# Two branch projections as three products of split operands in place of full fp32 products

## The chip, the cores and the metric

The kernel runs on one core of a Trainium2 chip. The metric is device time in microseconds (us), the median of several executions. One execution was also recorded by the hardware profiler; all rows below come from it. TensorE is called PE, its weight load PEld, VectorE DVE, ScalarE ACT, GpSimd POOL, SyncE SP.

## The reference, cut to what matters

Three layers run one after the other on 512 tokens of width 1024 (with 256 context tokens in the first two). Mixer A is a grouped attention with rotary positions, mixer B a neighbourhood attention; the third layer has two branches side by side, an mLSTM and a sparse attention, and merges them. Only this merge is touched:

```python
ya = sigmoid(p["m_o"]) * mh * silu(p["m_z"])          # 512 x 1024, from the mLSTM
yb = yn * silu(p["n_z"])                              # 512 x 512, from the sparse attention
merged = (sigmoid(p["g_a"]) * (ya @ w_branch_a[l])    # 1024 x 1024
          + sigmoid(p["g_b"]) * (yb @ w_branch_b[l])) # 512 x 1024
x = x + merged @ w_out[l]
```

512 tokens are eight selection blocks, fewer than the sixteen to be selected, so all are taken, and the sparse attention is, for a query tile, two causal attentions over the same past, plus a small one over compressed blocks.

## The kernel before, in words

**Layout.** Activations lie with features on partitions: 8 chunks k of 128 features, each 128x512. Weights come in "units" of 256 output columns (1 MB, eight chunks of 128x256), loaded by SP in the fixed order `UNITS` (line 56 on) into `W`, which holds two units in turn.

**Split products.** For most units the weight and the activation are each held in two parts, a high one rounded to fp32r and a low one, the remainder. ACT casts `W` into `WH` (line 1692), POOL subtracts to get `WL` (line 2431; DVE in a few places), in four pieces per unit. `WH` and `WL` too hold two units in turn (`PART`). The activation's parts lie in `H` (`HX`, `HC`) and `L` (`LX`, `LC`); `parts` makes them, with a cast on ACT (line 1742) and a subtraction on DVE (2038) or POOL (2472). A product over one chunk is then three fp32r matmuls (lines 1416 to 1418): high by high, high by low, low by high. `proj` is this product, `pj` the generator that emits it, eight chunks to one 128x512 output.

**Plain units.** Units named in `PLAIN` are not split: `x_wa` (line 1662, branch A: 4 units x 2 outputs x 8 chunks = 64 products) and `x_wb` (line 1672, branch B: 8 outputs x 4 chunks = 32 products) multiply `W` by the fp32 activation directly. The trace records two MATMULs for each of these full products.

**Order of work.** Every engine runs its part of one list, `plan`, in order; semaphores tie the engines together. `tick` emits the next waiting piece of a split at chunks 3 and 7 of an output, that is four times per unit. `tick` also emits the load of the unit after next when the fourth piece is out; for a plain unit the load is emitted when the unit's products are done. Within an attention (`careful`), a piece waits until its load is some work old.

**The sparse attention stage.** `attention("c", ...)` runs 32 steps (4 head pairs x 4 query tiles x 2 key sets). Step n emits its scores (line 1496), the softmax on DVE (max), ACT (exp) and POOL (scaling), then the output product of step n-2 (lines 1523, 1531) and the transposes of step n-1 (line 1506). There is one pair of score banks, so the scores of step n+1 wait for both exps of step n. Between, `fill_in` takes products from `gen_c`: 16 of gate unit `ga` j, 16 of `wa` j, for j = 0 to 3. Each step has two halves; a half with weight t takes products until the sum `spent` of their declared costs has reached

```python
until_ = spent[0] + (work - spent[0]) * todo[n][2] / left
```

A tile's weight is (tile+1)/2.5. A `ga` product declares 5.12, a `wa` product 9; `work` is 64 x (5.12 + 9) = 903.7.

**After it.** Eight outputs of gate units `gb` (64 products), then branch B with `x_wb` f = 0 to 7, each followed by a DVE multiply (2403), a DVE add (2406) and the parts of `mg` f; then `out_proj("wo")`, the last norm and the stores. `out_proj` starts with seven chunks of two outputs in turn, so chunk 7 of `mg` is needed late.

**The mLSTM.** Per head hd, projections `mq`, `mk`, `mv`, `mo`, `mz`; after some of them `do_later` emits one deferred piece of the head before (`m_den`, `m_var`, `m_scale`). `m_scale` ends with POOL writing `ya` (line 2531).

Of the kernel before, what the change touches and what calls it, by code (L numbers as in the profile page):

```python
# [8 lines left out]
ALU = mybir.AluOpType  # L9
# [63 lines left out]

UNITS = unit_order()
EARLY = [0, 4, 1, 5, 2, 6, 3, 7]
PLAIN = ("mod", "w1k", "w1v", "wa", "wb")
PART = [sum(u[0] not in PLAIN for u in UNITS[:n]) % 2 for n in range(len(UNITS))]


# [87 lines left out]
def build(nc, wu, vp, cc, cs1, xt, biasb, pos, out):  # L167
    ctx = ExitStack()
    with ctx:
# [116 lines left out]
        s_pcs, s_pc, s_pce, s_pct, s_pcT = (signal("cmp_" + n) for n in ("scores", "work", "exp", "turn", "turned"))  # L286
        s_nth, s_nz = signal("n_gate_tanh"), signal("n_gate")

        s_ga, s_wa, s_mg, s_gbt, s_wb, s_mgb, s_sum, s_fin = (signal("x_" + n) for n in ("ga", "wa", "merged_a", "gb", "wb", "merged_b", "merged", "final"))

        plan, before, last = [], {}, {}

        COST = {"proj": 0.6, "score": 1.0, "turn": 0.5, "pv": 0.7, "x_wa": 0.9, "mod_mm": 0.9, "m_qk": 0.9, "m_num": 1.0}
        done_work, loaded_at, careful = [0.0], {}, [False]

        def do(*item):
# [812 lines left out]
        def m_var(hd):  # L1111
            mps["var", hd] = bank(ONE.take(("mvar", hd), (s_vv, (hd,))))
            do("m_var", hd)

        def m_scale(hd):
            mps["hb", hd] = bank(ONE.take(("mhb", hd), (s_hs, (hd, 1))))
            do("m_scale", hd)

        for hd in range(4):
            conv("mq", hd)  # L1120
            do_later(hd)
            conv("mk", hd)
            do_later(hd)
            if hd == 0:
                do("m_decay")
            un = Unit("mv", hd)
            for s in range(4):
                o = bank(ONE.take(("mv", hd, s), (s_vh, (hd, s))))
                run(pjt(("mv", hd, s), un, s, "h", o))
                do("m_value", hd, s)  # L1130
            un.done(s_proj, "mv", hd, 3)
            do_later(hd)
            for nm_ in ("mo", "mz"):
                un = Unit(nm_, hd)
                for m in range(2):
                    g = (nm_, hd, m)
                    o = bank(ONE.take(g, (s_oth, (hd, m)) if nm_ == "mo" else (s_zg, (hd, m))))
                    run(pj(g, un, 0, T, 128 * m, "h", o))
                    do("m_gate", *g)
                un.done(s_proj, *g)  # L1140
                if nm_ == "mo":
                    if hd == 0:
                        for x, ev in (("g", s_gc), ("s", s_em), ("r", s_gb)):
                            mps["gcol", x] = bank(ONE.take(("gcol", x), (ev, ())))
                            do("m_gate_col", x)
                        do("m_gates_done")
                    mps["E", hd] = bank(ONE.take(("mE", hd), (s_ee, (hd, 3))))
                    do("m_exp", hd)
            for j in range(4):
                mps["qk", hd, j] = bank(ONE.take(("mqk", hd, j), (s_sw, (hd, j))))  # L1150
                do("m_qk", hd, j)
            for m in range(2):
                mps["num", hd, m] = bank(ONE.take(("mnum", hd, m), (s_num, (hd, m))))
                do("m_num", hd, m)
            do("m_num_sq", hd)
            later[:] = [lambda hd=hd: m_den(hd), lambda hd=hd: m_var(hd), lambda hd=hd: m_scale(hd)]

# [147 lines left out]
        def gen_c():  # L1307
            for j in range(4):
                un = Unit("ga", j)
                for m in range(2):  # L1310
                    g = ("ga", j, m)
                    o = bank(FC.take(g, (s_ga, (j, m))))
                    yield from pj(g, un, 0, T, 128 * m, "h", o)
                    do("x_ga", j, m)
                un.done(s_proj, "ga", j, 1)
                un = Unit("wa", j)
                for m in range(2):
                    wps["wa", j, m] = (un.n, bank(FC.take(("wa", j, m), (s_mg, (j, m)))))
                    for k in range(8):
                        if k % 4 == 3:  # L1320
                            tick()
                        do("x_wa", j, m, k)
                        yield 9
                    do("x_merge_a", j, m)
                un.done(s_wa, j, 1)

        def steps_c(pair):
            out_ = []
# [9 lines left out]
                    out_.append((lambda: True, make, (tile + 1) / 2.5))  # L1338
            return out_

        attention("c", [s for pair in range(4) for s in steps_c(pair)], SC, TC, PbC, PTbC, OC, gen_c(), 8 * 8 * (T / 100 + 9), lambda n: None)

# [3 lines left out]
        for j in range(4):  # L1348
            un = Unit("gb", j)
            for m in range(2):  # L1350
                g = ("gb", j, m)
                o = bank(ONE.take(g, (s_gbt, (2 * j + m,))))
                run(pj(g, un, 0, T, 128 * m, "h", o))
                do("x_gb", j, m)
                if j == 0 and m == 0:
                    rbroad("c", 0, R1)
                do("norm2_x", 2 * j + m)
            un.done(s_proj, "gb", j, 1)
        for jj in range(2):
            un = Unit("wb", jj)  # L1360
            for j in range(2):
                for m in range(2):
                    f = 4 * jj + 2 * j + m
                    tick()
                    wps["wb", f] = (un.n, j, m, bank(ONE.take(("wb", f), (s_mgb, (f,)))))
                    do("x_wb", f)
                    parts("m", f, 0, mg[:, f, :], [(s_sum, (f,)), (s_proj, ("gb", 3, 1))], "pool")
            un.done(s_wb, f)
        norm("e", Arena(), X_ONLY, [(s_wa, (3, 1))], lambda k, p: [(s_res, ("wo", k, 0))])
        out_proj("wo", None, XONLY, False, "m", ["e"])  # L1370
        close("e", 0, ONE)
        RE = bank(ONE.take("RE", (s_fin, (7,))))
# [26 lines left out]
        def tensor(e, w):  # L1399
            def proj(g, k):  # L1400
# [4 lines left out]
                w.wait_ge(*x_low(G.phase, k, int(G.lo >= T)))  # L1405
                f0, f1, part = 256 * k + G.f0, 256 * k + G.f0 + G.width, PART[G.unit]
                wh, wl = WH[:, part, f0:f1], WL[:, part, f0:f1]
                xh, xl = H.at(k, G.lo, G.hi), L.at(k, G.lo, G.hi)
                if G.by_tokens:
                    o = G.out[:, 0:G.width]  # L1410
                    e.matmul(o, xh, wh, start=(k == 0), stop=False)  # L1411
# [241 lines left out]
                    t = e.transpose(cps["turn", tile][:, 128 * g:128 * g + 128], pc[tile % 2][:, 128 * g:128 * g + 128], c("id"))  # L1653
                t.then_inc(*s_pct.by(tile))

            def x_wa(j, m, k):
                n, o = wps["wa", j, m]
                if k == 0:
                    free(w, ("wa", j, m))
                    w.wait_ge(*s_w[n % 2](n))  # L1660
                    w.wait_ge(*s_ya(3, 1))
                t = e.matmul(o, unit_w(n)[:, k, 128 * m:128 * m + 128], ya[:, k, :], start=(k == 0), stop=(k == 7))  # L1662
                if k == 7:
                    t.then_inc(*s_wa.by(j, m))

            def x_wb(f):
                n, j, m, o = wps["wb", f]
                free(w, ("wb", f))
                w.wait_ge(*s_w[n % 2](n))
                w.wait_ge(*s_post("c", 31))  # L1670
                for k in range(4):
                    t = e.matmul(o, unit_w(n)[:, 4 * j + k, 128 * m:128 * m + 128], nz[:, k, :], start=(k == 0), stop=(k == 3))  # L1672
                t.then_inc(*s_wb.by(f))

            program(e, w, dict(proj=proj, mod_mm=mod_mm, mod_tr=mod_tr, norm_sums=norm_sums, rbroad=rbroad, a_key_sums=a_key_sums,
                               a_key_norm=a_key_norm, a_key_rope=a_key_rope, a_query_sums=a_query_sums, a_query_turn=a_query_turn,
                               score=score, turn=turn, pv=pv, m_gates=m_gates, m_gate_col=m_gate_col, m_exp=m_exp, m_qk=m_qk,
                               m_num=m_num, m_den=m_den, m_var=m_var, m_scale=m_scale, n_rotate=n_rotate, n_hidden=n_hidden,
                               n_cmp_out=n_cmp_out, cmp=cmp, cmp_turn=cmp_turn, x_wa=x_wa, x_wb=x_wb))

        def scalar(e, w):
            def silu():
# [55 lines left out]
            def parts(phase, k, j):  # L1738
                src, after = partsrc[phase, k, j]
                lo, hi = FULL[j]  # L1740
                await_all(w, after)
                e.copy(H.at(k, lo, hi), src).then_inc(*s_xh.by(phase, k, j))

            def a_key_raw(m):
                w.wait_ge(*s_proj("ak", 1, 1))
# [208 lines left out]
        def vector(e, w):  # L1954
# [79 lines left out]
            def parts(phase, k, j):  # L2034
                if part_by[phase, k, j] == "dve":
                    lo, hi = FULL[j]
                    w.wait_ge(*s_xh(phase, k, j))
                    e.tensor_tensor(L.at(k, lo, hi), partsrc[phase, k, j][0], H.at(k, lo, hi).bitcast(F32), ALU.subtract).then_inc(*s_xl_dve.by(phase, k, j))

            def a_key_raw(m):  # L2040
                w.wait_ge(*s_ksq(m))
# [350 lines left out]
                e.scalar_tensor_tensor(out=nz[:, tile, :], in0=nz[:, tile, :], scalar=1.0, in1=groups["nz", tile].out, op0=ALU.add, op1=ALU.mult).then_inc(*s_nz.by(tile))  # L2392

            def x_merge_a(j, m):
                w.wait_ge(*s_wa(j, m))
                w.wait_ge(*s_ga(j, m))
                await_all(w, N_DONE)
                e.scalar_tensor_tensor(out=mg[:, 2 * j + m, :], in0=sg[m], scalar=1.0, in1=wps["wa", j, m][1], op0=ALU.add, op1=ALU.mult).then_inc(*s_mg.by(j, m))

            def x_wb(f):  # L2400
                w.wait_ge(*s_wb(f))
# [20 lines left out]
        def gpsimd(e, w):  # L2422
# [45 lines left out]
            def parts(phase, k, j):  # L2468
                if part_by[phase, k, j] == "pool":
                    lo, hi = FULL[j]  # L2470
                    w.wait_ge(*s_xh(phase, k, j))
                    e.tensor_tensor(L.at(k, lo, hi), partsrc[phase, k, j][0], H.at(k, lo, hi).bitcast(F32), ALU.subtract).then_inc(*s_xl_pool.by(phase, k, j))

            def a_key_sums():
                w.wait_ge(*s_kvar())
# [304 lines left out]
```

## Time and profile before

| what | value |
|---|---|
| median of 3 runs | 1638.17 us (1637.87 to 1638.43) |
| the profiled execution | 1637.83 us |
| its span, first to last instruction | 1636.1 us |
| mean granted TensorE clock | 0.975 |

The profiled execution's own time is 1.7 us above its span. A row of the trace gives start, duration, engine, line, operation, operands and count; "128*128 128x512" is the stationary tile and the moving one. The end of a MATMUL is modelled and includes its way through the array, so neighbouring MATMULs overlap: what one costs PE is the distance from its start to the next start, not its duration.

### The profile page before, as it was taken

To read this page: it belongs to the slowest core of one execution; us is meant where nothing else is said; L and a number is where in the kernel's file an instruction comes from. 1 tells how busy PE (TensorE), PEld (TensorE's weight loads), DVE (VectorE), ACT (ScalarE), POOL (GpSimd) and SP (SyncE) were. 2 spreads that over 40 slices of the span, in tenths; PEclk is the share of its full clock that TensorE was granted. 3 is DMA by queue.
4 is the path that set the end of the run, shared out by engine and by line. 5 is a ranking of instruction groups with operands and counts; after the bars stand their busy time and mean duration, and the time that the engine had idled before them with its cause. 6 is when DMAs were issued, how large, how long until landed. Compare 5 with 4: busy or idle time off the path is not lost.

```text
span 1636.1 us, 25018 instructions
## 1 busy us (share of the span) xinstructions
PE 1559.0 (95%) x9858; PEld 1216.3 (74%) x9858; DVE 733.9 (45%) x1707; ACT 622.4 (38%) x1301; POOL 656.7 (40%) x640
## 2 busy tenths in 40 slices
PE   5899999999898999999999899999999999999997
PEld 3787777777587888787867687878878865655755
DVE  4434555555534345444355563443424444456033
ACT  3244444444532433333344453433322343333221
POOL 2534334444532533434344453525346244333252
PEclk8999999999998999999999899999999999999998
DMA  9111111110132222322231122213122212110221
GB/s 396 36 71 53 44 36 52 52 53 27 53 108 99 82 75 77 110 79 104 78 123 47 61 103 73 86 52 103 52 77 78 91 65 78 52 52 26 78 99 56
DMA packets 22148, 128.20 MB, mean 78 GB/s; under 512 B 2448, under 2 KB 2576, under 8 KB 8080
## 3 DMA queue, kind: packets, MB, share of 16 engines
q1 hardware_dynamic: 21888, 126.35, 21.4%
q8 instruction: 78, 1.28, 0.3%
q14 instruction: 38, 0.31, 0.1%
q10 hardware_dynamic: 144, 0.26, 0.1%
HBM read 124.50 MB, written 2.10 MB: 77 GB/s over the span
## 4 chain that ended last, share of the span: by engine, by line
PE 85%; DVE 6%; ACT 3%; POOL 2%; issue 2%; DMA 1%; SPq 0%; POOLq 0%; DVEq 0%; ACTq 0%
PE PS L1416 16%; PE PS L1418 15%; PE PS L1417 15%; PE PS L1496 7%; PE PS L1506 6%; PE PS L1531 6%; PE PS L1662 3%; PE PS L1411 3%; PE PS L1412 3%; PE PS L1413 3%; PE PS L1672 2%; DVE sm L2110 1%; PE PS L1584 1%; PE PS L1576 1%; PE PS L1429 1%
## 5 line engine op out<-in xcount | busy, mean ns | idle before, releaser
L2431 POOL TENSOR_TENSOR WL<-W,WH 128x512 fp32r<-128x512 f32 x280 | 367.4, 1328 | 321.0 <-ACT WH L1692 320.5
L1416 PE MATMUL PS<-HX,WH 128*128 128x512 f32 x1008 | 421.3, 418 | 9.0 <-DVE LX L2031 3.1
L1418 PE MATMUL PS<-HX,WL 128*128 128x512 f32 x1008 | 399.9, 397 | 0.0
L1417 PE MATMUL PS<-LX,WH 128*128 128x512 f32 x1008 | 399.3, 396 | 0.0
L1416 PEld LDWEIGHTS PS<-HX,WH 128*128 128x128 f32 x1008 | 193.5, 192 | 60.0 <-issue 15.9
L1418 PEld LDWEIGHTS PS<-HX,WL 128*128 128x128 f32 x1008 | 192.7, 191 | 42.9
L1417 PEld LDWEIGHTS PS<-LX,WH 128*128 128x128 f32 x1008 | 193.5, 192 | 37.1 <-issue 3.4
L1692 ACT CAST WH<-W 128x512 fp32r<-128x512 f32 x296 | 172.1, 618 | 48.3 <-DMA W<-in_wu 22.2
L1778 ACT ACTIVATE AR<-PS,sm 128x768 f32<-128x768 f32 (+4 forms) x160 | 115.7, 723 | 171.2 <-DVE sm L2115 101.1
L2110 DVE TENSOR_REDUCE sm<-PS 128x1 f32<-128x512 f32 (+4 forms) x224 | 150.0, 670 | 54.3 <-PE PS L1496 49.7
L2498 POOL TENSOR_SCALAR AR<-AR,sm 128x768 f32<-128x768 f32 (+1 forms) x96 | 75.1, 782 | 186.3 <-DVE sm L2126 186.3
L1496 PE MATMUL PS<-AR 64*128 64x256 f32 (+3 forms) x704 | 124.3, 460 | 9.9 <-ACT XC L1778 4.0
L2498 POOL TENSOR_SCALAR XC<-XC,sm 128x512 f32<-128x512 f32 x64 | 45.0, 704 | 164.2 <-DVE sm L2126 164.2
L1496 PEld LDWEIGHTS PS<-AR 64*128 64x128 f32 x704 | 60.1, 187 | 67.3 <-issue 42.0
L1506 PE MATMUL PS<-C,AR 128*128 128x128 f32 x608 | 100.8, 283 | 7.5 <-DVE AR L2146 3.9
L1788 ACT COPY AR<-PS 128x512 f32<-128x512 f32 (+1 forms) x112 | 62.2, 555 | 118.8 <-PE PS L1506 118.1
L1778 ACT ACTIVATE XC<-PS,sm 128x512 f32<-128x512 f32 x64 | 44.2, 691 | 145.8 <-DVE sm L2115 145.8
L1506 PEld LDWEIGHTS PS<-C,AR 128*128 128x128 f32 x608 | 68.2, 140 | 41.0 <-issue 22.7
L1531 PEld LDWEIGHTS PS<-AR 128*64 128x64 f32 x1408 | 76.0, 137 | 28.3 <-issue 25.2
L1531 PE MATMUL PS<-AR 128*64 128x128 f32 x1408 | 95.4, 280 | 1.5 <-ACT AR L1788 1.2
L1411 PE MATMUL PS<-WH,HX 128*128 128x256 f32 x320 | 94.3, 295 | 0.8 <-POOL WL L2431 0.8
L1413 PE MATMUL PS<-WL,HX 128*128 128x256 f32 x320 | 90.5, 283 | 0.0
(273 smaller groups left out, 2472.6 us busy)
## 6 DMA issues: line engine op xcount, KB each, us to landing
W<-in_wu SPq DMA_DIRECT2D x98, 1024.0 KB, 4.8
AR<-in_wu SPq DMA_DIRECT2D x8, 1024.0 KB, 11.5
AR<-in_biasb SPq DMA_DIRECT2D x32, 256.0 KB, 2.7
XX<-in_xt SPq DMA_DIRECT2D x2, 1024.0 KB, 6.2
out<-XX SPq DMA_DIRECT2D x8, 256.0 KB, 2.2
XC<-in_xt SPq DMA_DIRECT2D x1, 1024.0 KB, 14.3
C<-in_cc SPq DMA_DIRECT2D x1, 770.5 KB, 8.7
CS<-in_cs SPq DMA_DIRECT2D x1, 512.0 KB, 9.6
```

What stands on the lines that cost most here:

```text
L1411: e.matmul(o, xh, wh, start=(k == 0), stop=False)
L1413: t = e.matmul(o, xh, wl, start=False, stop=(k == 7))
L1416: e.matmul(o, wh, xh, start=(k == 0), stop=False)
L1417: e.matmul(o, wh, xl, start=False, stop=False)
L1418: t = e.matmul(o, wl, xh, start=False, stop=(k == 7))
L1496: t = e.matmul(PS[:, s.score[h] + a:s.score[h] + b], l, r, start=True, stop=True)
L1506: t = e.transpose(o[:, j * 128:j * 128 + 128], s.pb[h][:, (q0 + j) * 128:(q0 + j) * 128 + 128], c("id"))
L1531: t = e.matmul(s.out[h], s.values[h][j], s.pt[h][:, j * 128:j * 128 + 128], start=(j == 0 and s.first), stop=(j == nv - 1 and s.final))
L1692: e.copy(WH[:, PART[n], a:z], W[:, n % 2, a:z]).then_inc(*s_wh.by(n, q))
L1778: e.activation(s.pb[h][:, 0:s.n], PS[:, s.score[h]:s.score[h] + s.n], ACT.Exp, bias=smn[:, i % 4:i % 4 + 1], scale=(1.0 if s.scale is None ...
L2110: e.tensor_reduce(mx, x, AX.X, ALU.max).then_inc(*s_max.by(name, n, h))
L2431: e.tensor_tensor(WL[:, d, a:z], W[:, n % 2, a:z], WH[:, d, a:z].bitcast(F32), ALU.subtract).then_inc(*s_wl_pool.by(n, q))
```

## The change

`wa` and `wb` leave `PLAIN`, so their units are split like the others. Branch A's products go through `pj` with phase "y": its high parts lie in `HC` and `LC`, its low parts in the place of `ya` itself, made by `parts_y`, a fourth deferred piece after each head, for which `do_later` is called once more per head. Branch B's products have phase "z": parts of `nz` j are made after `gb` j, high in `HC`, low in `LC`. `work` becomes 64 x 2 x 5.12 = 655.4, all products declaring 5.12. Every other `mg` low part moves from POOL to DVE. The short description of the change also names mixer A's scores as full products; they are full products in both versions (line 1496), and the diff does not touch them.

```diff
-PLAIN = ("mod", "w1k", "w1v", "wa", "wb")
+PLAIN = ("mod", "w1k", "w1v")
...
-        AR = sb("AR", [P, ASZ])
+
+        with nc.sbuf_tensor("AR", [P, ASZ], F32) as AR:
+            pass
+        ARp = sb("AR_parts", [P, ASZ], F32R)
...
+        HIGH = {"y": Blocks(HC[:, :], LCt[:, :]), "z": Blocks(HC[:, :])}
+        LOW = {"y": Blocks(ARp[:, 0:KC * T]), "z": Blocks(LCt[:, :])}
...
-        COST = {"proj": 0.6, "score": 1.0, "turn": 0.5, "pv": 0.7, "x_wa": 0.9, "mod_mm": 0.9, "m_qk": 0.9, "m_num": 1.0}
+        COST = {"proj": 0.6, "score": 1.0, "turn": 0.5, "pv": 0.7, "mod_mm": 0.9, "m_qk": 0.9, "m_num": 1.0}
...
+        def parts_y(hd):
+            for k in (2 * hd, 2 * hd + 1):
+                parts("y", k, 0, ya[:, k, :], [(s_ya, (hd, k % 2)), (s_proj, ("bv", 3, 5))], "dve")
...
                 if nm_ == "mo":
+                    do_later(hd)
...
-            later[:] = [lambda hd=hd: m_den(hd), lambda hd=hd: m_var(hd), lambda hd=hd: m_scale(hd)]
+            later[:] = [lambda hd=hd: m_den(hd), lambda hd=hd: m_var(hd), lambda hd=hd: m_scale(hd), lambda hd=hd: parts_y(hd)]
...
-                    wps["wa", j, m] = (un.n, bank(FC.take(("wa", j, m), (s_mg, (j, m)))))
-                    for k in range(8):
-                        if k % 4 == 3:
-                            tick()
-                        do("x_wa", j, m, k)
-                        yield 9
+                    g = ("wa", j, m)
+                    o = bank(FC.take(g, (s_mg, (j, m))))
+                    yield from pj(g, un, 0, T, 128 * m, "y", o)
                     do("x_merge_a", j, m)
-                un.done(s_wa, j, 1)
+                un.done(s_proj, "wa", j, 1)
...
-        attention("c", ..., gen_c(), 8 * 8 * (T / 100 + 9), lambda n: None)
+        attention("c", ..., gen_c(), 8 * 8 * 2 * T / 100, lambda n: None)
...
             un.done(s_proj, "gb", j, 1)
+            parts("z", j, 0, nz[:, j, :], [(s_post, ("c", 8 * j + 7)), (s_proj, ("wa", 3, 1))], "dve")
...
-                    parts("m", f, 0, mg[:, f, :], [(s_sum, (f,)), (s_proj, ("gb", 3, 1))], "pool")
+                    parts("m", f, 0, mg[:, f, :], [(s_sum, (f,)), (s_proj, ("gb", 3, 1))], "dve" if f % 2 else "pool")
...
-            def x_wa(j, m, k):
-                n, o = wps["wa", j, m]
-                if k == 0:
-                    free(w, ("wa", j, m))
-                    w.wait_ge(*s_w[n % 2](n))
-                    w.wait_ge(*s_ya(3, 1))
-                t = e.matmul(o, unit_w(n)[:, k, 128 * m:128 * m + 128], ya[:, k, :], start=(k == 0), stop=(k == 7))
...
             def x_wb(f):
                 n, j, m, o = wps["wb", f]
                 free(w, ("wb", f))
-                w.wait_ge(*s_w[n % 2](n))
-                w.wait_ge(*s_post("c", 31))
                 for k in range(4):
-                    t = e.matmul(o, unit_w(n)[:, 4 * j + k, 128 * m:128 * m + 128], nz[:, k, :], start=(k == 0), stop=(k == 3))
+                    w.wait_ge(*w_low(n, 2 * j + k // 2))
+                    w.wait_ge(*x_low("z", k, 0))
+                    a = 256 * (4 * j + k) + 128 * m
+                    wh, wl = WH[:, PART[n], a:a + 128], WL[:, PART[n], a:a + 128]
+                    xh, xl = high("z").at(k, 0, T), low("z").at(k, 0, T)
+                    e.matmul(o, wh, xh, start=(k == 0), stop=False)
+                    e.matmul(o, wh, xl, start=False, stop=False)
+                    t = e.matmul(o, wl, xh, start=False, stop=(k == 3))
```

`proj` and the three `parts` take their places from `high(phase)` and `low(phase)`, and the merge on DVE reads the output of the `wa` group. `Blocks` only cuts a tensor into 128x512 blocks.

## Rows read from the trace of the kernel before

**Rows 1.** The page, busy time of each engine, then the chain that ended last.

```profile
PE 1559.0 (95%) x9858; PEld 1216.3 (74%) x9858; DVE 733.9 (45%) x1707; ACT 622.4 (38%) x1301; POOL 656.7 (40%) x640
PE 85%; DVE 6%; ACT 3%; POOL 2%; issue 2%; DMA 1%; SPq 0%; POOLq 0%; DVEq 0%; ACTq 0%
```

**Rows 2.** Stretches; columns: length, busy PE, PEld, DVE, ACT, POOL, clock, DMA, GB/s.

```profile
1327.00:1503.00 176.00, 171.90 (x989) 102.48 (x989) 88.31 (x311) 63.58 (x186) 59.30 (x80) 1.00 0.14 52
1503.00:1547.50 44.50, 44.50 (x200) 36.95 (x201) 8.80 (x14) 10.20 (x19) 15.25 (x12) 1.00 0.20 71
1547.50:1575.20 27.70, 27.64 (x65) 11.96 (x63) 11.08 (x15) 6.83 (x12) 11.99 (x10) 1.00 0.12 39
1575.20:1636.00 60.80, 47.50 (x208) 38.85 (x208) 19.01 (x30) 12.05 (x22) 20.53 (x16) 0.90 0.23 87
```

**Rows 3.** Groups of instructions by form, PE: the full products of both branches.

```profile
L1662 PE MATMUL PS<-AR,W 128*128 128x512 f32 x128 | 62.1, 593 | 0.0
L1672 PE MATMUL PS<-AR,W 128*128 128x512 f32 x64 | 27.6, 592 | 0.0
```

**Rows 4.** Timeline of PE: the end of `gb`, branch B, the start of `wo`.

```profile
1540.03 0.39 PE L1416 MATMUL PS<-HX,WH 128*128 128x512 f32 x1
...
1547.28 0.39 PE L1418 MATMUL PS<-HX,WL 128*128 128x512 f32 x1
1547.51 27.63 PE L1672 MATMUL PS<-AR,W 128*128 128x512 f32 x64
1575.92 0.50 PE L1416 MATMUL PS<-HX,WH 128*128 128x512 f32 x1 [0.78 <-DVE AR L2403]
```

**Rows 5.** Timeline of the attention stage: scores of steps 18, 19, 20.

```profile
1429.63 0.70 PE L1496 MATMUL PS<-AR 64*128 64x256 f32 x4
1433.12 0.70 PE L1496 MATMUL PS<-AR 64*128 64x256 f32 x4
1436.90 0.92 PE L1496 MATMUL PS<-AR 64*128 64x384 f32 x4 [0.40 <-ACT AR L1778]
```

**Rows 6.** The same: scores of steps 28 and 29.

```profile
1478.84 0.92 PE L1496 MATMUL PS<-AR 64*128 64x384 f32 x4 [0.40 <-ACT AR L1778]
...
1483.23 0.59 PE L1496 MATMUL PS<-AR 64*128 64x384 f32 x2 [0.36 <-ACT AR L1778]
```

**Rows 7.** The chain of waits in order of time: scores of steps 1 and 2.

```profile
1330.63 0.42 PE PS L1496 x4
...
1334.19 0.63 PE PS L1496 x4
```

**Rows 8.** Who waited for whom, PE, whole run: total us, times, longest.

```profile
PE PS L1496 <- ACT AR L1778: 3.9, 8, 0.8
PE PS L1416 <- POOL WL L2431: 0.8, 1, 0.8
```

**Rows 9.** The page: lows and casts of weights, exps, the weight load to landing.

```profile
L2431 POOL TENSOR_TENSOR WL<-W,WH 128x512 fp32r<-128x512 f32 x280 | 367.4, 1328 | 321.0 <-ACT WH L1692 320.5
L1692 ACT CAST WH<-W 128x512 fp32r<-128x512 f32 x296 | 172.1, 618 | 48.3 <-DMA W<-in_wu 22.2
L1778 ACT ACTIVATE AR<-PS,sm 128x768 f32<-128x768 f32 (+4 forms) x160 | 115.7, 723 | 171.2 <-DVE sm L2115 101.1
...
W<-in_wu SPq DMA_DIRECT2D x98, 1024.0 KB, 4.8
```

**Rows 10.** Timeline of ACT and DVE around the start of branch B.

```profile
1547.71 0.60 ACT L1945 ACTIVATE AR<-PS 128x512 f32<-128x512 f32 x1 [4.84 <-PE PS L1418]
1552.59 0.62 ACT L1742 CAST HX<-AR 128x512 fp32r<-128x512 f32 x1 [4.29 <-DVE AR L2406]
...
1551.87 0.69 DVE L2406 TENSOR_TENSOR AR<-AR 128x512 f32<-128x512 f32 x1
```

**Rows 11.** Timeline of POOL and ACT at the end of the mLSTM.

```profile
1244.07 2.56 POOL L2531 TENSOR_TENSOR AR<-AR 128x512 f32<-128x512 f32 x2 [2.70 <-DVE AR L2321]
1249.59 0.60 ACT L1896 ACTIVATE AR<-PS 128x512 f32<-128x512 f32 x1 [5.62 <-PE PS L1418]
```

**Rows 12.** A stretch of the mLSTM; columns as in Rows 2.

```profile
1175.00:1225.00 50.00, 50.00 (x270) 41.24 (x269) 14.62 (x27) 15.62 (x29) 24.18 (x23) 1.00 0.26 85
```

More of the change, by code:

```diff
@@ L204, in at, with __init__, high, low @@
                 return self.x[:, k, lo:hi] if lo < T else self.y[:, k, lo - T:hi - T]
+        class Blocks:
+            def __init__(self, *places):
+                self.blocks = [p[:, T * k:T * k + T] for p in places for k in range(p.shape[1] // T)]
+            def at(self, k, lo, hi):
+                return self.blocks[k][:, lo:hi]
         xT = Rows(XX[:, :], XC[:, :])
         H, L = Rows(HX[:, :], HC[:, :]), Rows(LX[:, :], LCt[:, :])
+        HIGH = {"y": Blocks(HC[:, :], LCt[:, :]), "z": Blocks(HC[:, :])}
+        LOW = {"y": Blocks(ARp[:, 0:KC * T]), "z": Blocks(LCt[:, :])}
+        def high(phase):
+            return HIGH.get(phase, H)
+        def low(phase):
+            return LOW.get(phase, L)
         class Arena:
@@ L287, in build @@
         s_nth, s_nz = signal("n_gate_tanh"), signal("n_gate")
-        s_ga, s_wa, s_mg, s_gbt, s_wb, s_mgb, s_sum, s_fin = (signal("x_" + n) for n in ("ga", "wa", "merged_a", "gb", "wb", "merged_b", "merged", "final"))
+        s_ga, s_mg, s_gbt, s_wb, s_mgb, s_sum, s_fin = (signal("x_" + n) for n in ("ga", "merged_a", "gb", "wb", "merged_b", "merged", "final"))
         plan, before, last = [], {}, {}
-        COST = {"proj": 0.6, "score": 1.0, "turn": 0.5, "pv": 0.7, "x_wa": 0.9, "mod_mm": 0.9, "m_qk": 0.9, "m_num": 1.0}
+        COST = {"proj": 0.6, "score": 1.0, "turn": 0.5, "pv": 0.7, "mod_mm": 0.9, "m_qk": 0.9, "m_num": 1.0}
         done_work, loaded_at, careful = [0.0], {}, [False]
@@ L1339, in steps_c @@
             return out_
-        attention("c", [s for pair in range(4) for s in steps_c(pair)], SC, TC, PbC, PTbC, OC, gen_c(), 8 * 8 * (T / 100 + 9), lambda n: None)
+        attention("c", [s for pair in range(4) for s in steps_c(pair)], SC, TC, PbC, PTbC, OC, gen_c(), 8 * 8 * 2 * T / 100, lambda n: None)
         ar = Arena(16 * T + 4 * T)
@@ L1366, in build @@
                     do("x_wb", f)
-                    parts("m", f, 0, mg[:, f, :], [(s_sum, (f,)), (s_proj, ("gb", 3, 1))], "pool")
+                    parts("m", f, 0, mg[:, f, :], [(s_sum, (f,)), (s_proj, ("gb", 3, 1))], "dve" if f % 2 else "pool")
             un.done(s_wb, f)
-        norm("e", Arena(), X_ONLY, [(s_wa, (3, 1))], lambda k, p: [(s_res, ("wo", k, 0))])
+        norm("e", Arena(), X_ONLY, [(s_proj, ("wa", 3, 1))], lambda k, p: [(s_res, ("wo", k, 0))])
         out_proj("wo", None, XONLY, False, "m", ["e"])
@@ L1407, in proj @@
                 wh, wl = WH[:, part, f0:f1], WL[:, part, f0:f1]
-                xh, xl = H.at(k, G.lo, G.hi), L.at(k, G.lo, G.hi)
+                xh, xl = high(G.phase).at(k, G.lo, G.hi), low(G.phase).at(k, G.lo, G.hi)
                 if G.by_tokens:
@@ L1654, in cmp_turn @@
                 t.then_inc(*s_pct.by(tile))
-            def x_wa(j, m, k):
-                n, o = wps["wa", j, m]
-                if k == 0:
-                    free(w, ("wa", j, m))
-                    w.wait_ge(*s_w[n % 2](n))
-                    w.wait_ge(*s_ya(3, 1))
-                t = e.matmul(o, unit_w(n)[:, k, 128 * m:128 * m + 128], ya[:, k, :], start=(k == 0), stop=(k == 7))
-                if k == 7:
-                    t.then_inc(*s_wa.by(j, m))
             def x_wb(f):
@@ L1678, in tensor @@
                                m_num=m_num, m_den=m_den, m_var=m_var, m_scale=m_scale, n_rotate=n_rotate, n_hidden=n_hidden,
-                               n_cmp_out=n_cmp_out, cmp=cmp, cmp_turn=cmp_turn, x_wa=x_wa, x_wb=x_wb))
+                               n_cmp_out=n_cmp_out, cmp=cmp, cmp_turn=cmp_turn, x_wb=x_wb))
         def scalar(e, w):
@@ L1741, in parts @@
                 await_all(w, after)
-                e.copy(H.at(k, lo, hi), src).then_inc(*s_xh.by(phase, k, j))
+                e.copy(high(phase).at(k, lo, hi), src).then_inc(*s_xh.by(phase, k, j))
             def a_key_raw(m):
@@ L2037, in parts @@
                     w.wait_ge(*s_xh(phase, k, j))
-                    e.tensor_tensor(L.at(k, lo, hi), partsrc[phase, k, j][0], H.at(k, lo, hi).bitcast(F32), ALU.subtract).then_inc(*s_xl_dve.by(phase, k, j))
+                    e.tensor_tensor(low(phase).at(k, lo, hi), partsrc[phase, k, j][0], high(phase).at(k, lo, hi).bitcast(F32), ALU.subtract).then_inc(*s_xl_dve.by(phase, k, j))
             def a_key_raw(m):
@@ L2394, in x_merge_a @@
             def x_merge_a(j, m):
-                w.wait_ge(*s_wa(j, m))
+                w.wait_ge(*s_proj("wa", j, m))
                 w.wait_ge(*s_ga(j, m))
                 await_all(w, N_DONE)
-                e.scalar_tensor_tensor(out=mg[:, 2 * j + m, :], in0=sg[m], scalar=1.0, in1=wps["wa", j, m][1], op0=ALU.add, op1=ALU.mult).then_inc(*s_mg.by(j, m))
+                e.scalar_tensor_tensor(out=mg[:, 2 * j + m, :], in0=sg[m], scalar=1.0, in1=groups["wa", j, m].out, op0=ALU.add, op1=ALU.mult).then_inc(*s_mg.by(j, m))
             def x_wb(f):
@@ L2471, in parts @@
                     w.wait_ge(*s_xh(phase, k, j))
-                    e.tensor_tensor(L.at(k, lo, hi), partsrc[phase, k, j][0], H.at(k, lo, hi).bitcast(F32), ALU.subtract).then_inc(*s_xl_pool.by(phase, k, j))
+                    e.tensor_tensor(low(phase).at(k, lo, hi), partsrc[phase, k, j][0], high(phase).at(k, lo, hi).bitcast(F32), ALU.subtract).then_inc(*s_xl_pool.by(phase, k, j))
             def a_key_sums():
```

## The prediction

> **What bounds the kernel now.** I read the page's busy times and chain first: PE is busy 95% of the span and carries 85% of the chain that ended last, so time follows PE wherever PE is really full [rows 1]. The four stretches in which the changed work lies come next [rows 2]. In `gb` (1503 to 1547.5) and branch B (to 1575.2) PE is busy throughout, DVE, ACT and POOL at most 43%. In the attention stage (1327 to 1503) PE shows 171.9 of 176 us, but this flatters it: the ends of matmuls are modelled, so small holes are covered. The last stretch holds `wo` and the closing norm. The granted clock is 1.00 in the first three stretches, the level of 2.4 GHz, so the prices below need no correction.
>
> **Price of a product, both ways.** A split product: from the start at 1540.03 to the start at 1547.51 are 33 matmuls of lines 1416 to 1418, 7.48 / 33 = 0.2267 us each, three of them 0.680 us [rows 4]. A full product: 64 records for 32 products begin at 1547.51; the group lasts 27.63 us with the last one's 0.592 us, so 63 distances take 27.04 us, 0.4292 each and 0.858 a product [rows 3, 4]. Branch A's 128 records have the same duration (593 against 592 ns), so the same price [rows 3]. The gain is 0.178 us a product; 64 + 32 = 96 products give 17.1 us if PE bounds all of them.
>
> The Trainium skill (FP8 and Floating Point Precision, TensorE Precision Notes) describes true fp32 as four passes through the array, high and low parts each by each. By that count three of four passes would stay and a product would cost 0.75 x 0.858 = 0.644 us; that is 96 x 0.215 = 20.6 us in all, 3.5 us more than the rows give. The rows do not quite agree: a quarter of a full product is 0.215 us and a matmul of the split one 0.227, and I go by the rows.
>
> **Branch B (32 products).** PE has no wait inside this stretch [rows 2, 4], so 32 x 0.178 = 5.7 us go. Added waits: chunk 3 of the new parts "z" follows the last `gb` output. ACT's tanh starts 0.2 us after that output's last matmul is replaced on PE and takes 0.60, a cast takes 0.62 and DVE's subtraction about 0.69 [rows 10]; from 1547.51 that is 0.2 + 0.6 + 0.6 + 0.7 = 2.1 us, and PE comes to chunk 3 after 3 x 0.68 = 2.04. I put 0.2 us for the hand-over (bounds 0 and 1). Its cover is thin, but what is queued behind the waiting matmul is only branch B itself. The weights' lows: `wb` 0 is split during `gb` 3, `wb` 1 during the first four outputs of `wb` 0, `wo` 0 during the next four, `wo` 1 during `wo` 0. A low piece takes POOL 1.33 us [rows 9], with the half of the `mg` parts left to POOL 1.33 + 0.65 = 2.0 us per output, and an output now lasts 4 x 0.68 = 2.72. Four lows leave POOL in time; DVE has 0.69 x 2.5 = 1.7 us per output. The start of `wo` waited 0.78 us for DVE's merge of the last output [rows 4]; that stays. Branch B: -5.5.
>
> **Attention stage (64 products).** If PE bounded every step: 64 x 0.178 = 11.4 us. Some steps are bound otherwise. Scores wait for the exps of the step before: step 19 (scores at 1433.12) lasts 3.78 us and ends with a wait on ACT, step 28 lasts 4.39 and ends so too [rows 5, 6]; in all PE waited 3.9 us at this place, eight times (in the whole run) [rows 8]. These durations are floors of a step, about 3.4 to 3.8 us for the two narrow tiles and 4.4 for the third; step 18 lasted 3.49 without a marked wait [rows 5].
> I then worked the filling rule through for both versions. Before, a `wa` product declares 9 and a `ga` product 5.12, and each half step rounds up, so products are spent early: steps 0 and 1 take 4 each, and the last pair (steps 24 to 31) is left 17, namely 2, 2, 2, 2, 2, 2, 3, 2. After, with 5.12 for all, steps of tile 0 take 2, of tile 1 4, of tile 2 6 and later 4, of tile 3 8, then 6, and the last pair 2, 2, 2, 2, 4, 4, 4, 2 = 22. Two effects follow. Steps 28 and 29 have 4 products, 2.72 us in place of 1.72, and step 19 has 4 too, so the waits there, about 0.5 us each, are filled: +1.6 us. Other steps fall to the floor. Steps 0 and 1 lasted about 3.56 [rows 7] with four products, 2.7 us; with two they need 2.2 us of PE and get 3.4, a loss of 1.2 us each. Steps 26 and 27 keep two products, now 1.36 us in place of 1.72, and can't use it: 0.35 each; 9, 17 and 25 lose 0.1 or 0.2 each, and the last step 0.35. Together about 3.9 lost and 1.6 found, 2.3 net. Branch A: -11.4 + 2.3 = -9.1. Bounds: nothing lost (-11.4) and a third of the stage's gain only (-4), if the chain is nearer than these steps show.
>
> **New work on the other engines.** Six more units are split: 24 casts of 0.62 us on ACT and 24 lows of 1.33 on POOL [rows 9]. Sixteen of each fall into the attention stage: 9.9 us on ACT, now at 63.6 of 176, and 21.3 on POOL, now at 59.3 [rows 2]. There is room, but a cast can stand in front of an exp, a low in front of a scaling. ACT was idle 171.2 us before 160 exps, 1.07 us before each [rows 9], so most of it fits; I put 0.5 us for the stage (bounds 0 and 3). Parts "y" are eight casts and eight subtractions of 0.69 over the mLSTM, where PE is busy throughout while ACT is at 31% and DVE at 29% [rows 12]. The last of them waits for `ya` (3, 1), written by POOL at 1246.6, while ACT reaches it at 1249.6 + 0.6 [rows 11]: no wait. For earlier heads it stands one projection unit, 16 products or 10.9 us, behind `m_scale`. I cost it at nothing; uncovered it would be 16 x 0.65 = 10 us, which nothing in the rows suggests. Loads: a plain unit's successor was loaded only when its products were done, a split unit's when its fourth piece is out, so loads of 4.8 us [rows 9] come earlier; cost nothing.
>
> **Sum.** -5.5 - 9.1 + 0.5 = -14.1. The profiled execution took 1637.83 us (span 1636.1 and 1.7 around it), 0.34 below the median. 1637.83 - 14.1 = 1623.7 us, and by the median 1624.1; I predict 1623.8.
>
> **The rivals.**
> *Full gain.* PE bounds every step, the small holes close: 1637.8 - 17.1 = 1620.7, or a little less where the better spread fills waits as well. For it: in the chain most pieces of the stage are PE's. Against: the waits of [rows 5, 6]. Chance 0.2.
> *The softmax chain takes over.* More than the narrow steps are at their floor, or casts and lows lengthen it; branch A brings 4 us or less: 1637.8 - 5.5 - 4 = 1628.3, down to nothing from branch A, 1632. For it: DVE and ACT serve both heads in turn there, and ACT gets more casts. Against: scores waited for an exp only eight times [rows 8], and the wide tiles' steps hold six to eight products, 4 us and more beside the attention's own matmuls. Chance 0.16.
> *Weights' lows come late, slower than before.* The place is the first chunk of each of the six new split units: cast and low of a piece follow one another, 4 x 1.33 + 0.62 = 5.9 us for a unit, plus 4.8 of load when the ring runs dry. Over 17.1 / 6 = 2.9 us of it open per unit turn the sign; all of it open is 35 - 17 = 18 us, 1656. Against: of 280 lows now made, PE's matmuls of line 1416 waited for one, 0.8 us [rows 8]. Chance 0.03.
> *The change does not do what it says*, that is, PE's stream is no shorter because semaphores and weight loads at each chunk eat 0.18 us: 1637. In `gb`, whose chunks carry the same waits, the distances are even 0.227, which speaks against it. Chance 0.02.
> *Three passes of four*, the page's count as this kernel's price: 1637.8 - 20.6 = 1617.2. The measured distances exclude it but for the unseen. Chance 0.02.
>
> **Numbers.** My forecast, 1622 to 1627, has 0.57. The range for 8 in 10 reaches from full gain to the middle of the chain rival: 1619.5 to 1630. Less than 0.2% (3.3 us) is about what a measurement of this kernel can tell from no change. Faster by more than that 0.94, within 0.03, slower 0.03.
>
> **What would show it.** Right: between starts of lines 1416 to 1418 in branch B 0.227 us, from the end of `gb` to the start of `wo` 32 x 0.68 + 0.2 + 0.8 = 22.8 us in place of 28.4; the attention stage some 167 us in place of 176; waits on ACT's exp at steps 0, 1, 26 and 27, none at 28 and 29; the mLSTM and `gb` of the same length. Wrong: PE waiting on POOL's lows in `wa` or `wb` units, or an attention stage that keeps more than 170 us, or an mLSTM that grew.

## The result, and the profile after

The changed kernel takes 1622.0 us (median of 4 runs, 1617.3 to 1625.6) against 1638.0 (4 runs, 1637.1 to 1638.4): ratio 0.9901, 95% interval 0.9874 to 0.9929. Run again in the experiments it gave 1622.9 (6 runs) against 1637.7 (11 runs), ratio 0.9901, interval 0.9883 to 0.9919. The prediction was 1623.8, within 1619.5 to 1630. The profiled execution took 1620.71 us, span 1619.0.

The page of the changed kernel, to be read beside [rows 1, 9]: busy time by engine, the granted clock in 40 slices, the lows and casts of weights.

```profile
PE 1539.4 (95%) x9954; PEld 1229.6 (76%) x9954; DVE 747.5 (46%) x1723; ACT 639.8 (40%) x1337; POOL 685.0 (42%) x660
...
PEclk9999999999999999999998899999999999999998
...
L2450 POOL TENSOR_TENSOR WL<-W,WH 128x512 fp32r<-128x512 f32 x304 | 400.3, 1332 | 328.8 <-ACT WH L1711 328.2
...
L1711 ACT CAST WH<-W 128x512 fp32r<-128x512 f32 x320 | 186.8, 618 | 37.4 <-PE PS L1437 21.1
```

PE has 96 records more (three for two, 96 times) and is busy 20 us less. There are 24 casts and 24 lows more, at the price that each had before. PE stays the bound.

Branch B in the changed kernel, timeline of PE, beside [rows 4]:

```profile
1535.81 0.39 PE L1689 MATMUL PS<-HC,WH 128*128 128x512 f32 x1
1536.03 0.39 PE L1690 MATMUL PS<-LC,WH 128*128 128x512 f32 x1
1536.26 0.39 PE L1691 MATMUL PS<-HC,WL 128*128 128x512 f32 x1
...
1537.62 0.39 PE L1691 MATMUL PS<-HC,WL 128*128 128x512 f32 x1
1537.89 0.50 PE L1689 MATMUL PS<-HC,WH 128*128 128x512 f32 x1
1538.23 0.40 PE L1690 MATMUL PS<-LC,WH 128*128 128x512 f32 x1
...
1559.00 0.50 PE L1440 MATMUL PS<-HX,WH 128*128 128x512 f32 x1 [1.05 <-DVE AR L2422]
```

The matmuls follow one another at 0.227 us. At chunk 3, where the last part "z" is needed, the distances are 0.27 and 0.34, together 0.15 us more. From the first matmul of branch B to the first of `wo` it is 23.2 us in place of 28.4.

The attention stage, timeline of PE, beside [rows 5 to 7]: scores of steps 0 to 2, then of steps 24 to 28.

```profile
1322.74 0.49 PE L1520 MATMUL PS<-AR 64*128 64x128 f32 x4
1325.98 0.49 PE L1520 MATMUL PS<-AR 64*128 64x128 f32 x4 [0.32 <-ACT AR L1797]
1328.84 0.70 PE L1520 MATMUL PS<-AR 64*128 64x256 f32 x4 [0.61 <-ACT AR L1797]
...
1450.56 0.49 PE L1520 MATMUL PS<-AR 64*128 64x128 f32 x4
1454.97 0.49 PE L1520 MATMUL PS<-AR 64*128 64x128 f32 x4 [0.25 <-ACT AR L1797]
1458.49 0.70 PE L1520 MATMUL PS<-AR 64*128 64x256 f32 x4 [0.18 <-ACT AR L1797]
1461.96 0.70 PE L1520 MATMUL PS<-AR 64*128 64x256 f32 x4 [0.43 <-ACT AR L1797]
1465.74 0.92 PE L1520 MATMUL PS<-AR 64*128 64x384 f32 x4 [0.71 <-ACT AR L1797]
```

Steps 0, 1 and 24 to 27 have two products each, and each ends with a wait for an exp. Step 1 lasts 2.86 us, step 27 3.78, exactly what step 19 lasted before [rows 5]. PE's waits for an exp in the stage, total, times and longest, before and then changed:

```profile
PE PS L1496 <- ACT AR L1778: 1.6, 4, 0.5
PE PS L1520 <- ACT AR L1797: 3.4, 10, 0.7
```

The ten are the ends of steps 0, 1, 8, 9, 16, 17 and 24 to 27.

For comparing kernels I use stretches, cut at rows that every version has: the first scan of the mLSTM and the last rotation before the sparse attention (both DVE), the first score maximum of the stage (DVE), the first and the last tanh of `gb` (ACT), the first matmul of `wo` (PE), and the start of the last output of the closing norm. The marks of the changed kernel, timeline of DVE:

```profile
968.38 2.22 DVE L2285 TENSOR_TENSOR_SCAN AR<-AR,XC 4x512 f32<-4x512 f32 x1
...
1281.95 0.69 DVE L2349 TENSOR_TENSOR AR<-PS,CS 128x512 f32<-128x512 f32 x1 [0.60 <-PE PS L1640]
...
1324.19 0.29 DVE L2129 TENSOR_REDUCE sm<-PS 128x1 f32<-128x128 f32 x1
```

and timeline of ACT:

```profile
1496.98 0.60 ACT L1964 ACTIVATE AR<-PS 128x512 f32<-128x512 f32 x1 [5.90 <-PE PS L1442]
...
1536.01 0.60 ACT L1964 ACTIVATE AR<-PS 128x512 f32<-128x512 f32 x1 [3.81 <-PE PS L1442]
```

| stretch, us | before | before, again | changed | changed, again |
|---|---|---|---|---|
| start to the first scan | 970.6 | 971.6 | 968.4 | 970.6 |
| scan to the last rotation | 313.5 | 313.6 | 313.6 | 313.6 |
| rotation to the first score maximum | 43.7 | 42.0 | 42.2 | 42.2 |
| attention | 180.88 | 180.95 | 172.79 | 172.85 |
| `gb` | 39.02 | 39.02 | 39.02 | 39.02 |
| branch B, to `wo` | 28.21 | 28.21 | 22.99 | 22.96 |
| `wo` and the end | 56.78 | 56.56 | 56.56 | 56.54 |

The two stretches that hold the changed products give 8.1 + 5.2 = 13.3 us and repeat within 0.1. The profiled pair lies 17.1 apart. Of the other 3.8 us 2.2 arose before the first scan, where no line of the diff acts, and 1.5 between rotation and first score maximum, where TensorE's clock fell to half in one execution and not in the other (shown under "The kernel before again"). The last 0.2 (all three are rounded) lies in the closing norm, where eight small matmuls of line 1447 took 1.27 us at a granted clock of 0.77; in the changed kernel they took 1.05 at full clock.

### The profile page after: what moved, and what is told of

The parts are those of the page before. It is cut to its first block, busy times and chain, and to the rows that moved or that the text cites. A ratio compares the mean times of both kernels' runs of the same rounds, so it can differ in the third digit from the quotient of the medians.

```text
span 1619.0 us, 25305 instructions
## 1 busy us (share of the span) xinstructions
PE 1539.4 (95%) x9954; PEld 1229.6 (76%) x9954; DVE 747.5 (46%) x1723; ACT 639.8 (40%) x1337; POOL 685.0 (42%) x660
## 4 chain that ended last, share of the span: by engine, by line
PE 83%; DVE 8%; ACT 3%; issue 3%; POOL 2%; DMA 1%; SPq 0%; POOLq 0%; DVEq 0%; ACTq 0%
PE PS L1440 16%; PE PS L1442 15%; PE PS L1441 15%; PE PS L1520 7%; PE PS L1530 6%; PE PS L1555 6%; PE PS L1435 3%; PE PS L1436 3%; PE PS L1437 3%; DVE sm L2129 1%; PE PS L1608 1%; PE PS L1600 1%; PE PS L1453 1%; POOL WL L2450 1%; DMA XC<-in_xt 1%
## 5 line engine op out<-in xcount | busy, mean ns | idle before, releaser
L2450 POOL TENSOR_TENSOR WL<-W,WH 128x512 fp32r<-128x512 f32 x304 | 400.3, 1332 | 328.8 <-ACT WH L1711 328.2
L1440 PE MATMUL PS<-HX,WH 128*128 128x512 f32 x1008 | 420.5, 417 | 11.4 <-DVE LX L2050 3.5
L1711 ACT CAST WH<-W 128x512 fp32r<-128x512 f32 x320 | 186.8, 618 | 37.4 <-PE PS L1437 21.1
L1520 PE MATMUL PS<-AR 64*128 64x256 f32 (+3 forms) x704 | 124.4, 460 | 11.3 <-ACT AR L1797 5.7
L1440 PE MATMUL PS<-HC,WH 128*128 128x256 f32 (+1 forms) x304 | 94.8, 312 | 0.5 <-POOL LC L2474 0.5
```

The source lines that it names most:

```text
L1440: e.matmul(o, wh, xh, start=(k == 0), stop=False)
L1520: t = e.matmul(PS[:, s.score[h] + a:s.score[h] + b], l, r, start=True, stop=True)
L1711: e.copy(WH[:, PART[n], a:z], W[:, n % 2, a:z]).then_inc(*s_wh.by(n, q))
L2450: e.tensor_tensor(WL[:, d, a:z], W[:, n % 2, a:z], WH[:, d, a:z].bitcast(F32), ALU.subtract).then_inc(*s_wl_pool.by(n, q))
```

## The experiments

My theory: PE's stream sets the time; a split product costs 0.68 us against 0.86; in the attention stage part of the gain is lost in narrow steps, which the softmax chain holds at a floor; new work on ACT and POOL has room. The rivals are those of the prediction.

**The changed kernel again.**

> The changed kernel once more, to see how its time scatters. Both theories: 1617 to 1626 us against 1638. If the scatter comes from TensorE's clock, the runs with the lower mean granted clock are the longer ones, and the stretches of the attention and of branch B (171 and 23.2 us in the first profile) do not change.

1622.9 us. The stretches are in the table. By mean granted clock the six runs were 1624.0 and 1624.5 at 0.974, 1623.0 at 0.975, 1622.8 at 0.977, 1618.5 at 0.980, 1617.3 at 0.982: the scatter of 7 us goes with the clock. The 11 runs of the kernel before, beside them, go the same way, from 1640.1 at 0.971 to 1633.8 at 0.980. A straight line through the 17 times against the clock, with one slope for both kernels, falls 0.74 us per 0.001 and puts the gain at equal clock at 13.8 us, give or take 0.7 (an estimate from these runs): what the stretches say.

**Branch B alone.** `wb` out of `PLAIN` with the new `x_wb` and every other low part of `mg` on DVE, branch A as before.

```diff
-PLAIN = ("mod", "w1k", "w1v", "wa", "wb")
+PLAIN = ("mod", "w1k", "w1v", "wa")
```

> Branch B alone in split products, branch A as full products with the old declared costs. My theory: 32 products at 0.178 us less, a small hand-over wait, so 5.2 us less than before (ratio 0.9968), from the end of gb to the start of wo 23.2 us in place of 28.4, attention stage as before (176 us). Rival (weights' lows or the start of wo give it back): under 2 us less.

1630.2 us, ratio 0.9947 (0.9931 to 0.9963). Attention 180.88, branch B 22.98. The start of `wo`:

```profile
1570.41 0.50 PE L1435 MATMUL PS<-HX,WH 128*128 128x512 f32 x1 [1.04 <-DVE AR L2427]
```

Branch B gives its 5.2 us and nothing is handed back. The ratio says 8.7 us (6.1 to 11.3); the runs of this kernel had a mean clock of 0.978, those of before 0.974. At equal clock, reckoned as above, it is 5.9 us, give or take 1.1.

**Branch A alone.** The changed kernel with `wb` plain, the old `x_wb` and all low parts of `mg` on POOL.

```diff
-PLAIN = ("mod", "w1k", "w1v")
+PLAIN = ("mod", "w1k", "w1v", "wb")
```

> Branch A alone in split products, branch B as full products. My theory: 8.5 to 9.5 us less than before (ratio 0.9945), all of it in the attention stage, 28.4 us between gb and wo. Rival (PE bounds every step): 11.4 us less. Rival (the softmax chain takes over): 4 us or less.

1625.6 us, ratio 0.993 (0.9914 to 0.9946). Attention 172.80, branch B 28.21, as in before to the hundredth. Branch A gives 8.1 us: neither 11.4 nor 4. The two halves of the change do not touch each other.

**A fourth matmul in each product.**

```diff
                     e.matmul(o, wh, xl, start=False, stop=False)
-                    t = e.matmul(o, wl, xh, start=False, stop=(k == 3))
+                    e.matmul(o, wl, xh, start=False, stop=False)
+                    t = e.matmul(o, wl, xl, start=False, stop=(k == 3))
```

and the same in `proj` for phase "y".

> The changed kernel with a fourth fp32r matmul, low part by low part, in each of the 96 products. My theory: a product costs 4 x 0.227 = 0.907 us, more than a full product's 0.858, so branch B's stretch grows from 23.2 to 30.3 us (before: 28.4), and the whole is 18 to 21 us above the changed kernel and 3 to 5 above before. Rival (a full product is four passes at the price of the split one's three, so four matmuls cost as much as a full product): the time of before, branch B's stretch 28.4 us.

1643.4 us, ratio 1.0036 (1.0022 to 1.0049), slower than before and 20.5 us above the changed kernel. Timeline of PE in branch B of this kernel:

```profile
1553.46 0.39 PE L1691 MATMUL PS<-HC,WH 128*128 128x512 f32 x1
1553.68 0.39 PE L1692 MATMUL PS<-LC,WH 128*128 128x512 f32 x1
1553.91 0.39 PE L1693 MATMUL PS<-HC,WL 128*128 128x512 f32 x1
1554.14 0.39 PE L1694 MATMUL PS<-LC,WL 128*128 128x512 f32 x1
1554.36 0.39 PE L1691 MATMUL PS<-HC,WH 128*128 128x512 f32 x1
...
1579.79 0.50 PE L1440 MATMUL PS<-HX,WH 128*128 128x512 f32 x1 [0.78 <-DVE AR L2425]
```

A product of four takes 0.90 us, the full one 0.86 [rows 4]. Branch B's stretch is 29.75 us, 6.8 above the changed kernel and 1.5 above before; attention 186.8, 14.0 above the changed kernel (64 x 0.227 = 14.5 if nothing hides). By the stretches this kernel stands 7.4 us above before, by the medians 5.7, both more than the 3 to 5 expected. The Trainium skill (FP8 and Floating Point Precision, TensorE Precision Notes) counts four passes for true fp32; no row here shows passes, only two records for a full product. In price a full product is not four of this kernel's fp32r matmuls: it is 5% cheaper than four. So 3/4 is not the ratio of the prices here; it is 0.680 / 0.858 = 0.79.

**Even fill.** The changed kernel, fill of the sparse attention spread by an absolute budget.

```diff
                     until_ = spent[0] + (work - spent[0]) * todo[n][2] / left
+                    if name == "c":
+                        until_ = work * (1 - (left - todo[n][2]) / sum(2 * t[2] for t in todo)) - 1e-6
...
-                    out_.append((lambda: True, make, (tile + 1) / 2.5))
+                    out_.append((lambda: True, make, (1.5, 2.0, 2.0, 2.5)[tile]))
```

> The changed kernel, but the fill of the sparse attention is spread against an absolute budget: 3, 3, 4, 4, 4, 4, 5, 5 products in the eight steps of every pair, in place of 2, 2, 4, 4, 6, 6, 8, 6 in the first and 2, 2, 2, 2, 4, 4, 4, 2 in the last. My theory (narrow steps at the softmax floor ate 2 to 3 us of branch A's gain): the marked holes in the changed kernel's narrow steps, some 5 us in all, close; from the first score maximum to the first tanh of gb 168 to 170 us in place of 172.8. Rival (what is missing of 11.4 us went to per-product overhead or to casts and lows in the way): 172 to 173.

1616.9 us, ratio 0.9878 (0.9862 to 0.9893): faster than before. It did not run beside the changed kernel; that it beats that one too rests on the stretches. Attention 167.13, 5.7 less than the changed kernel's and below the 168 to 170 expected. Its scores of steps 25 to 27, to be held against those of the changed kernel above:

```profile
1449.49 0.49 PE L1522 MATMUL PS<-AR 64*128 64x128 f32 x4
1453.39 0.70 PE L1522 MATMUL PS<-AR 64*128 64x256 f32 x4
1457.74 0.70 PE L1522 MATMUL PS<-AR 64*128 64x256 f32 x4
```

No wait is marked: steps with three and four products are longer (3.9 and 4.4 us) but PE has no hole in them, and the wide steps are shorter for it.

**Even fill, full products.** The same two edits on the kernel before, and `yield T / 100` with the new `work` for `wa`.

> The kernel before, full products in both branches, with the same even spread of products over the steps. My theory: before had only some 2 us of such holes, so the stretch goes from 180.9 to about 178.7 us, and stands 10 to 11 us above the changed kernel with the even spread, the full gain of 64 products. Rival (overhead): the distance of the two even kernels is 8 us as in the pair of before and after.

1633.3 us, ratio 0.998 (0.997 to 0.9991). Attention 177.45, so before had 3.4 us of such holes, not 2. The two even kernels stand 177.45 - 167.13 = 10.3 us apart, the pair of before and after 8.1. With the holes gone from both, 64 products bring 10.3 of 11.4 us; the split change by itself had opened 2.2 us more of holes than before had. The last 1.1 us are spread over all steps. Step 5 has four `wa` products in both even kernels. With full products:

```profile
1347.69 0.92 PE L1498 MATMUL PS<-AR 64*128 64x384 f32 x4
...
1351.55 1.88 PE L1664 MATMUL PS<-AR,W 128*128 128x512 f32 x4
1353.37 1.13 PE L1498 MATMUL PS<-AR 64*128 64x512 f32 x4
```

With split products:

```profile
1346.47 0.92 PE L1522 MATMUL PS<-AR 64*128 64x384 f32 x4
...
1348.21 0.48 PE L1442 MATMUL PS<-HC,WH 128*128 128x512 f32 x1
1348.53 0.39 PE L1443 MATMUL PS<-AR_parts,WH 128*128 128x512 f32 x1
1348.76 0.40 PE L1444 MATMUL PS<-HC,WL 128*128 128x512 f32 x1
...
1351.51 0.70 PE L1522 MATMUL PS<-AR 64*128 64x512 f32 x2
```

The step lasts 5.68 us and 5.04, 0.64 for four products: 0.16 each in place of 0.178. Over the whole stage of the even kernel, the first matmul of a run of split products, behind the attention's own matmuls, stands 0.315 us before the next, the others 0.232, where branch B has 0.227. How much of the 1.1 us each of the two makes up is not shown.

**All low parts of `mg` on POOL.**

```diff
-... "dve" if f % 2 else "pool")
+... "pool")
```

> The changed kernel with all low parts of mg on POOL, as before. My theory: POOL has 2 x 1.3 = 2.6 us per output of 2.72 and just keeps up, DVE's last merge comes earlier, the wait at the start of wo falls from 1.05 to 0.8 us, and the time from gb to the end stays within 0.5 us. Rival (POOL is too slow for it, which the move to DVE cured): wo waits for POOL, 1 to 3 us longer.

1622.8 us, ratio 0.9908 (0.9891 to 0.9926). The start of `wo`:

```profile
1562.75 0.50 PE L1440 MATMUL PS<-HX,WH 128*128 128x512 f32 x1 [0.78 <-DVE AR L2422]
```

The wait is 0.78 again, branch B 22.68 us, 0.3 shorter. `wo` and the end are 56.96, 0.4 longer, but that is the clock: from the first matmul of `wo` to the closing norm's first it is 47.10 us in both, and that norm's eight small matmuls take 1.46 us here,

```profile
1609.85 1.46 PE L1471 MATMUL PS<-C,AR 128*128 128x1 f32 x8 [2.17 <-DVE AR L1998]
```

at a granted clock of 0.67, against 1.05 at full clock in the changed kernel. So the move to DVE costs 0.3 us and cures nothing.

**Every low of `wa` and `wb` made twice.**

```diff
+                    if UNITS[n][0] in ("wa", "wb"):
+                        e.tensor_tensor(WL[...], W[...], WH[...].bitcast(F32), ALU.subtract).then_inc(*s_twice.by(n, q))
+                        w.wait_ge(*s_twice(n, q))
```

> The changed kernel with every low part of a wa or wb unit made twice in a row on POOL, 24 subtractions of 1.33 us more. My theory (POOL's new work has room): attention stage 172.9 us to 173.5, from the last tanh of gb to the last merge 22.3 to 23. Rival (weights' lows are on the edge): each late low is paid on PE, 5 us and more of the added 32.

1622.3 us (1620.0 to 1628.8), ratio 0.9924 (0.9893 to 0.9954). The added lows, all instructions of their line (shortest, median and longest in ns, first and last start):

```profile
L2452 POOL TENSOR_TENSOR WL<-W,WH x24: 1267/1283/1748, 1335.2 to 1557.5; 128x512 fp32r<-128x512 f32 x24
```

PE's wait for a low in branch B, from the waits after 1300 us (total, times, longest):

```profile
PE PS L1690 <- POOL WL L2454: 1.3, 1, 1.3
```

31 us more on POOL cost 0.3 us in the attention (173.14) and 1.3 in branch B (24.31). `wo` and the end are 0.7 longer, 0.6 of it again in the closing norm's eight small matmuls (1.67 us at a granted clock of 0.58). Branch B had less room than I allowed, the attention as much.

**Every cast of `wa` made twice.**

```diff
+                if UNITS[n][0] == "wa":
+                    e.copy(WH[:, PART[n], a:z], W[:, n % 2, a:z]).then_inc(*s_twice.by(n, q))
+                    w.wait_ge(*s_twice(n, q))
```

> The changed kernel with every cast of a wa unit made twice in a row on ACT, 16 casts of 0.62 us and as many waits more in the attention stage. My theory (casts fit between exps except in narrow steps): attention stage 172.9 to 174.5 us. Rival (the softmax chain, ACT in it, bounds the stage): 5 to 10 us more.

1624.6 us (1618.3 to 1625.5), ratio 0.9933 (0.9909 to 0.9958). Attention 172.82: ten microseconds more on ACT cost nothing. The casts do not hold up the stage.

**The kernel before again.**

> The kernel before once more, for its profile. If the half-clock stretch at 1303 us belongs to its instruction stream it is there again; if it hangs on the phase in which the clock is looked at, it is absent in some profiles of this kernel and present in some of the changed one.

1637.1 us. The same stretch of 16 us in four profiles; columns: length, busy PE and its instructions, clock, DMA share, GB/s. The kernel before, as first profiled:

```profile
1296.00:1312.00 16.00, 15.67 (x98) 0.79 0.30 117
```

The kernel before, again:

```profile
1296.00:1312.00 16.00, 14.73 (x121) 1.00 0.35 129
```

The changed kernel, again:

```profile
1296.00:1312.00 16.00, 14.15 (x116) 1.00 0.31 114
```

The changed kernel with the even fill:

```profile
1296.00:1312.00 16.00, 15.67 (x98) 0.79 0.31 111
```

The half-clock stretch comes and goes. Of the four profiles with branch A in full products three have it, of the eight with branch A split three; it was there in the first profile of before and not in the first of the changed kernel. With it, the time from the last rotation to the first score maximum is 43.7 us, in one profile 44.5, without it 42.0 to 42.2. The time to the first scan, all of it in code that the versions share, lies between 966.1 and 971.6 us in the twelve profiles.

## Why the prediction was right

**Price of a product.** Right: 0.227 us a matmul in branch B of the changed kernel. In the four-part kernel the distances are 0.227 too; its branch B grew by 6.8 us and not by 32 x 0.227 = 7.3 because the wait at the start of `wo` fell from 1.05 to 0.78 and the hand-over was covered.

**Branch B, -5.5.** Measured -5.2. The hand-over at chunk 3 cost about 0.15, where 0.2 was put. What I had kept constant moved: the wait at the start of `wo` is 1.05 us in place of 0.78, because the odd parts of `mg`, now on DVE, stand before its last merges. All on POOL, the wait is back at 0.78.

**Branch A, -9.1 + 0.5.** Measured -8.1. The steps came out as the filling rule gave them: 2, 2, 4, 4, 6, 6, 8, 6 products in the first pair and no hole at steps 28 and 29. The sizes were off. The holes were larger on both sides: 3.4 us in before, where I found 1.6, and 5.7 after, where I had 3.9. Their difference, 2.2 to 2.3, came out, but partly by luck, since errors in single steps cancel. I read 3.56 us for steps 0 and 1 alike; that is step 1, step 0 lasted 4.20. With two products they took 3.24 and 2.86, under the floor of 3.4 that I used. Held against the same steps of the even fill, less one product each, they have some 1.1 us of hole in all (an estimate), not 2.4. Steps 8, 16 and 24 I did not count at all. Step 24 before, from its scores to those of step 25, lasted 4.40 us with two full products:

```profile
1463.57 0.49 PE L1496 MATMUL PS<-AR 64*128 64x128 f32 x4
...
1467.97 0.49 PE L1496 MATMUL PS<-AR 64*128 64x128 f32 x4
```

With two split ones it lasts 4.41 (1450.56 to 1454.97), so nothing is gained there. The 0.5 us for casts and lows in the way is not there: doubling the casts cost nothing, doubling the lows 0.3. And 1.1 us of the 64 products is missing even without holes.

**Parts "y", nothing.** Right in effect. Timeline of DVE at the last of them:

```profile
1248.57 2.40 DVE L2057 TENSOR_TENSOR AR_parts<-AR,LC 128x512 fp32r<-128x512 f32 x2 [1.07 <-ACT LC L1761]
1250.89 0.67 DVE L2349 TENSOR_TENSOR AR<-PS,CS 128x512 f32<-128x512 f32 x1
```

They hold up the rotation behind them, and PE does not wait for it: from the first scan to the last rotation both versions take 313.5 to 313.6 us, and from there to the first score maximum 42.0 to 42.2 where the clock is full.

**The sum.** 8.1 + 5.2 = 13.3 us against 14.1 predicted. The medians differ by 15 to 16; that the predicted 1623.8 lay so near 1622 is partly owed to the clock, which is luck. What makes the mean clock of these runs of the changed kernel 0.977 and that of before beside them 0.974 stays open: with the even fill both had 0.976 to 0.977, which speaks for chance, but it was not settled.

**The signs.** None of the signs of being wrong came: PE did not wait for a low of a `wa` or `wb` unit, the mLSTM did not grow, and the attention stage, cut as the prediction cut it, takes 176 - 8.1 = 167.9 us, under 170. The 171 us in the expectation of the first rerun is a wider cut, from 1320 to 1491 in the first profile of the changed kernel.

**The rivals.** Full gain: out, 8.1 of 11.4 in the attention. The softmax chain: there in the steps with two products, worth 2.2 us net, as the sum had it, not 7. Lows late: out, even doubled they cost 1.7 us in all. No effect: out. Three of four passes: out, by the distances and by the four-part kernel.

## What to carry to other kernels

Price a matmul by the distance between starts in a stretch where PE never waits; its recorded duration (0.39 us for the split matmul, 0.59 for each half of the full one) would have given 1.17 against 1.18, no gain at all. When filler work becomes cheaper, look at the steps it fills: those already at the floor of another chain keep their length, and the gain has to be moved to steps that can use it. Here spreading the same products evenly was worth 5.7 us with split products and 3.4 with full ones.

## What the runs showed of the hardware that was not expected

TensorE's clock falls to half at places that differ between executions of one kernel. In profiles of the same instruction stream the 6.8 us at half clock near 1303 us is there in some and absent in others, with PE's starts equal to 0.03 us up to that point (the first profile of before against the second of the changed kernel, reckoned from the last rotation). It costs 1.5 to 1.7 us here, less than its length, since PE at full clock then waits for lows; the second profile of the changed kernel has such a wait of 1.5 us at 1311.5. Over a whole run the time goes with the mean clock by up to 7 us (1617.3 at 0.982, 1624.5 at 0.974), more than the 5.2 us that branch B is worth. Attention, `gb` and branch B, cut at fixed rows, repeat to 0.1 us.
